# Hybrid decoder layer on one core: layer norm in seven spaced steps, input products and combined blocks at other places of the plan, rotation in four instructions

## The reference, cut to what matters

```
h = rmsnorm(x, norm_g)
p = einsum('btd,dn->btn', h, w_in)          # all branches read one projection
o_a = silu(a_z) * (a_b * dwconv3(a_c * a_u))
rq = rotary(r_q, pos);  rk = rotary(r_k, pos) * 128 ** -0.5
   # rotary: concat([x1*cos - x2*sin, x1*sin + x2*cos]), x1, x2 the halves of the head
o_r = silu(r_z) * head_norm(retention_chunked(rq, rk, r_v, S))
conv_c = dwconv31(glu_v * sigmoid(glu_g)) + bias
o_c = silu(c_z) * silu(layernorm(conv_c, ln_c_g, ln_c_b))
o_m = silu(m_z) * head_norm(sigmoid(m_o) * mlstm_chunked(...))
y = einsum(sum_n sigmoid(g_n) * (o_n @ w_br[n]), w_out);  x + y, final rmsnorm
```

## Time and profile before

| what | value |
|---|---|
| device time, median of 3 runs | 1559.46 us (1557.69 to 1561.15) |
| time of the profiled execution | 1561.5 us |
| span of the profiled execution | 1559.7 us |
| TensorE busy | 1506.2 us, 97% |
| VectorE busy | 916.5 us, 59% |
| ScalarE busy | 497.8 us, 32% |
| GpSimd busy | 673.9 us, 43% |
| mean granted clock of TensorE | 0.984 |

### The profile page before, as it was taken

The page is one execution under the profiler, slowest core; times in us unless marked ns, Lnnn a source line. Parts: engine busy times, 40 slices in busy tenths (PEclk is TensorE's granted clock), DMA queues, the critical chain, the costliest instruction groups (busy, mean ns, idle before and its releaser), DMA issues.

```text
span 1559.7 us, 26832 instructions
## 1 busy us (share of the span) xinstructions
PE 1506.2 (97%) x10433; PEld 1465.7 (94%) x10433; DVE 916.5 (59%) x1796; ACT 497.8 (32%) x989; POOL 673.9 (43%) x488
## 2 busy tenths in 40 slices
PE   8899999999999999989999999999889999999998
PEld 7899999999999999989999999999779999999886
DVE  6552442456767643277787688787654423885532
ACT  5333323222223233233333333333453331221211
POOL 4221212122132231386777677777546754662100
PEclk9999999999999999999999999999999999999999
DMA  4121212122121221312232222222222466655321
GB/s 170 46 96 41 72 40 84 57 69 73 41 73 34 80 79 42 121 50 87 83 100 82 71 74 70 90 79 88 69 91 68 163 206 203 204 182 158 116 81 71
DMA packets 63989, 144.38 MB, mean 93 GB/s; under 512 B 7656, under 2 KB 36344, under 8 KB 63736
## 3 DMA queue, kind: packets, MB, share of 16 engines
q1 hardware_dynamic: 56616, 116.62, 23.1%
q0 software_dynamic: 6048, 21.73, 3.9%
q10 hardware_dynamic: 1200, 4.33, 0.7%
HBM read 107.01 MB, written 35.64 MB: 91 GB/s over the span
## 4 chain that ended last, share of the span: by engine, by line
PE 79%; DVE 14%; issue 2%; ACT 2%; POOL 1%; DMA 0%; DVEq 0%; ACTq 0%; POOLq 0%
PE bank L1132 10%; PE bank L1134 10%; PE bank L1133 10%; PE bank L1083 8%; PE bank L1085 8%; PE bank L1084 8%; PE bank L1150 4%; PE bank L1151 4%; PE bank L1152 4%; PE bank L1339 2%; PE bank L1340 2%; PE bank L1341 2%; DVE xt L1875 1%; PE sums_ps L1280 1%; PE sums_ps L1270 1%
## 5 line engine op out<-in xcount | busy, mean ns | idle before, releaser
L1083 PE MATMUL bank<-h_hi,w_hi 128*128 128x352 f32 x1032 | 346.7, 336 | 7.5 <-DVE h_lo L1854 4.3
L1085 PE MATMUL bank<-h_hi,w_lo 128*128 128x352 f32 x1032 | 334.9, 324 | 0.0
L1084 PE MATMUL bank<-h_lo,w_hi 128*128 128x352 f32 x1032 | 334.5, 324 | 0.0
L1711 POOL TENSOR_TENSOR w_lo<-stage,w_hi 128x1024 fp32r<-128x1024 f32 x45 | 107.8, 2396 | 336.1 <-ACT w_hi L1381 336.0
L1711 POOL TENSOR_TENSOR t_lo<-stage,t_hi 128x512 fp32r<-128x512 f32 x140 | 187.7, 1343 | 142.9 <-ACT t_hi L1381 142.7
L1132 PE MATMUL bank<-h_hi,t_hi 128*128 128x264 f32 x864 | 248.0, 287 | 0.0
L1133 PE MATMUL bank<-h_lo,t_hi 128*128 128x264 f32 x864 | 246.5, 285 | 0.0
L1134 PE MATMUL bank<-h_hi,t_lo 128*128 128x264 f32 x864 | 246.0, 285 | 0.0
L1132 PE MATMUL bank<-c_hi,t_hi 128*128 128x264 f32 x648 | 187.7, 290 | 19.0 <-DVE part L2004 16.8
L1083 PEld LDWEIGHTS bank<-h_hi,w_hi 128*128 128x128 f32 x1032 | 196.8, 191 | 9.0 <-DVE h_lo L1854 4.6
L1084 PEld LDWEIGHTS bank<-h_lo,w_hi 128*128 128x128 f32 x1032 | 197.3, 191 | 0.1
(11 more groups left out here) (341 smaller groups left out, 2881.2 us busy)
## 6 DMA issues: line engine op xcount, KB each, us to landing
stage<-in_wa SPq DMA_DIRECT2D x64, 512.0 KB, 3.4
piece<-g_rows SPq DMA_DIRECT2D x96, 176.0 KB, 2.8
stage<-in_wg SPq DMA_DIRECT2D x32, 512.0 KB, 3.5
g_rows<-sgt SPq DMA_DIRECT2D x112, 132.0 KB, 1.8
o_raw<-o_rows SPq DMA_DIRECT2D x16, 528.0 KB, 6.9
stage<-in_wb SPq DMA_DIRECT2D x32, 256.0 KB, 2.7
xr<-in_xtok SPq DMA_DIRECT2D x9, 512.0 KB, 3.6
xt<-in_xT SPq DMA_DIRECT2D x6, 704.0 KB, 8.6
```

Of the source, the lines that this page charges most:

```text
L1083: pe.matmul(out, hi, h_hi[:, k, tok(b)], start=(k == 0), stop=False)
L1084: pe.matmul(out, hi, h_lo[:, k, tok(b)], start=False, stop=False)
L1085: mm = pe.matmul(out, lo, h_hi[:, k, tok(b)], start=False, stop=(k == KD - 1))
L1711: pool.tensor_tensor(lo, split_src(item), hi.bitcast(F32), ALU.subtract).then_inc(lo_done, 1)
```

## The change

The change has five parts. (1) In the retention phases `comb` moves from slots 1, 3, ..., 11 to 12, 13, ..., 17, and `comb_split` from 14, 16, 18 to 18, 20, 22. In the last phase `comb` 3 moves from 22..27 to 1, 3, ..., 11, `comb_split` to 14, 16, 18 and `comb4` from 31, 33, 35, 37 to 24, 27, 30, 33; attention 7 has stride 1.4 for 1.5. (2) `rotate` takes four instructions for six: a second table `tab2` holds sin and -sin, so that one multiplication and one addition cover all 128 partitions. It is one more DMA in GpSimd's queue, and as `tab2` overlaps the place of a later buffer GpSimd waits there for all attention state updates. (3) GLU 2 and 3 move from windows 9 and 14 to 6 and 10; conv_a and out_a of groups 1 to 3 move with them (out_a 3 to window 19). (4) The slots for taps change: none in slot 0 behind a window that is not a gate pair; behind an `acau` window 2, 6, 10, 11, 12, 13 for 0, 2, 6, 10, 12. Worked out from the lists, tap 1 of the four groups moves from (0, 1), (4, 6), (10, 0), (15, 0) to (0, 1), (5, 1), (9, 6), (14, 6), and `tap_s` from (1, 2), (5, 11), (10, 12), (15, 12) to (1, 6), (5, 13), (10, 6), (15, 5). (5) The layer norm starts at (19, 0), takes seven steps a block, at slots 0 `ln0`, 3 `lnm`, 4 `ln1`, 7 `ln1b`, 10 `lnv`, 11 `lns`, 13 `ln2`, with 14 slots from block to block, and `ln3a` and `ln3` lie five slots apart. Root and inverse stay in PSUM.

```diff
         if h:
             for i in range(6):
-                tasks.setdefault(2 * i + 1, []).append(("comb", h - 1, i))
+                tasks.setdefault(12 + i, []).append(("comb", h - 1, i))
             for c in range(3):
-                tasks.setdefault(14 + 2 * c, []).append(("comb_split", h - 1, c))
+                tasks.setdefault(18 + 2 * c, []).append(("comb_split", h - 1, c))
...
-    tasks = spread(attention(7), 0, 1.5)
+    tasks = spread(attention(7), 0, 1.4)
     for i in range(6):
-        tasks.setdefault(22 + i, []).append(("comb", 3, i))
+        tasks.setdefault(2 * i + 1, []).append(("comb", 3, i))
+    for c in range(3):
+        tasks.setdefault(14 + 2 * c, []).append(("comb_split", 3, c))
     for k in range(4):
-        tasks[31 + 2 * k] = [("comb4", k)]
-    for c in range(3):
-        tasks.setdefault(28 + c, []).append(("comb_split", 3, c))
+        tasks.setdefault(24 + 3 * k, []).append(("comb4", k))
...
-    for what in (glu(1), None, conv_a(0), None, out_a(0), None, conv_a(1), None, out_a(1), glu(2), None, conv_a(2), None,
-                 out_a(2), glu(3), None, conv_a(3), None, out_a(3), None, None, None, None, out_c(0), out_c(2),
+    for what in (glu(1), None, conv_a(0), None, out_a(0), None, glu(2), None, conv_a(1), None, glu(3), None, out_a(1),
+                 conv_a(2), None, out_a(2), None, conv_a(3), None, out_a(3), None, None, None, out_c(0), out_c(2),
...
-        short = bool(pairs) and pairs[-1][0] == "acau"
-        free = {"cvcg": (0, 1, 5, 6, 9, 10, 13), "acau": (0, 1, 2, 5, 6, 9, 10), "abaz": (0, 1, 2, 5, 6)}.get(
-            kind[0], (0, 2, 6, 10, 12) if short else (0, 1, 2, 5, 6, 9, 10, 11, 12, 13))
+        before = pairs[-1][0] if pairs else None
+        free = {"cvcg": (0, 1, 5, 6, 9, 10), "acau": (0, 1, 2, 5, 6, 9, 10), "abaz": (0, 1, 2, 5, 6)}.get(
+            kind[0], (2, 6, 10, 11, 12, 13) if before == "acau" else (0, 1, 2, 5, 6, 9, 10, 11, 12, 13))
+        if before != "g":
+            free = free[1:] if free[0] == 0 else free
...
     for b in range(3):
-        tasks_at(at + 9 * b, ("ln0", b))
-        tasks_at(at + 3 + 9 * b, ("ln1", b))
-        tasks_at(at + 6 + 9 * b, ("ln2", b))
+        for late_by, step in ((0, "ln0"), (3, "lnm"), (4, "ln1"), (7, "ln1b"), (10, "lnv"), (11, "lns"), (13, "ln2")):
+            tasks_at(at + 14 * b + late_by, (step, b))
     for g in range(4):
-        tasks_at(at + 28 + 3 * g, ("ln3", g))
+        tasks_at(at + 42 + 5 * g, ("ln3a", g))
+        tasks_at(at + 44 + 5 * g, ("ln3", g))
...
                 if pair == 0:
+                    if w == 0:
+                        pool.wait_ge(upd_done, 16)
...
-                    pool.dma_start(tab[:, :], rot).then_inc(tab_in, 16)
+                    pool.dma_start(tab[:, :], rot[0]).then_inc(tab_in, 16)
+                    pool.dma_start(tab2[:, :], rot[1]).then_inc(tab_in, 16)
...
-                c, s = tab[0:hw, tok(b)], tab[hw:P, tok(b)]
-                own(TT(dst[0:hw, :], ps[0:hw, :], c, ALU.mult))
-                own(TT(rb[0:hw, :], ps[hw:P, :], s, ALU.mult))
-                own(TT(dst[hw:P, :], ps[0:hw, :], s, ALU.mult))
-                TT(rb[hw:P, :], ps[hw:P, :], c, ALU.mult).then_inc(freed["V"], 1)
-                own.wait()
-                own(TT(dst[0:hw, :], dst[0:hw, :], rb[0:hw, :], ALU.subtract))
+                own(TT(dst[:, :], ps[:, :], tab[:, tok(b)], ALU.mult))
+                own(TT(rb[0:hw, :], ps[hw:P, :], tab2[hw:P, tok(b)], ALU.mult))
+                TT(rb[hw:P, :], ps[0:hw, :], tab2[0:hw, tok(b)], ALU.mult).then_inc(freed["V"], 1)
+                own.wait()
                 dve.wait_ge(freed["V"], n)
-                own(TT(dst[hw:P, :], dst[hw:P, :], rb[hw:P, :], ALU.add))
+                own(TT(dst[:, :], dst[:, :], rb[:, :], ALU.add))
...
             def ln2(b):
                 dve.wait_ge(ln_act, 2 * b + 2)
-                own(dve.reciprocal(lnr[:, :], lnr[:, :]))
+                own(dve.reciprocal(pb[:, 0:BLK], pb[:, 0:BLK]))
                 own.wait()
                 for g in range(4):
-                    own(TT(cc[g][:, tok(b)], cc[g][:, tok(b)], lnr[:, :], ALU.mult))
+                    own(TT(cc[g][:, tok(b)], cc[g][:, tok(b)], pb[:, 0:BLK], ALU.mult))
```

More of the change, by code:

```diff
@@ L202, in make_plan @@
     nw = len(pairs)
-    room[0] = room[0][1:]
     first_pair = {("cvcg", g): w for w, (kind, g, _) in enumerate(pairs) if kind == "cvcg"}
@@ L608, in hybrid_step @@
         kx = at("kx", [P, NB, P], F32, e_at + 544)
+        tab2 = at("tab2", [P, T], F32, e_at + 4640)
         v1 = sb("v1", [P, P + 1])
@@ L1298, in pt, with lnm @@
                     pe.transpose(tb[:, 0:NS], rt[0:NS, CH, 0:P], ident[0:NS, 0:NS]).then_inc(pt_ready, 1)
-            def ln1(b):
+            def lnm(b):
                 pe.wait_ge(pt_used, 24)
@@ L1305, in ln1, with lnv @@
                 pe.matmul(tb[:, 0:BLK], ones[:, :], lnsq[:, 0, :], start=True, stop=True).then_inc(ln_pe, 1)
-            def ln2(b):
+            def lnv(b):
                 pe.wait_ge(ln_dve, 4 * b + 3)
@@ L1312, in _ @@
             walk({"blk": blk, "prod": prod, "pblk": pblk, "m1": m1, "m3": m3, "m4": m4, "m5": m5, "m6": m6, "m7": m7, "mws": mws,
-                  "a": a, "b": b, "as": as_, "bs1": bs1, "bs2": bs2, "pt": pt, "ln1": ln1, "ln2": ln2})
+                  "a": a, "b": b, "as": as_, "bs1": bs1, "bs2": bs2, "pt": pt, "lnm": lnm, "lnv": lnv})
             ring = bank + [tb, pb]
@@ L1637, in ln1, with lns, ln3a @@
                 act.sem_inc(ln_act, 1)
-            def ln2(b):
+            def lns(b):
                 act.wait_ge(ln_pe, 2 * b + 2)
-                act.activation(lnr[:, :], pb[:, 0:BLK], ACT.Sqrt, bias=eps[:, :]).then_inc(ln_act, 1)
-            def ln3(g):
+                act.activation(pb[:, 0:BLK], pb[:, 0:BLK], ACT.Sqrt, bias=eps[:, :]).then_inc(ln_act, 1)
+            def ln3a(g):
                 act.wait_ge(ln_dve, 12 + g)
@@ L1662, in _ @@
                   "mws": mws, "a": a, "b": b, "as": as_, "bs1": bs1, "pr": pr, "tap0": tap0,
-                  "ln1": ln1, "ln2": ln2, "ln3": ln3})
+                  "ln1": ln1, "lns": lns, "ln3a": ln3a})
             act.wait_ge(acc_final, 1)
@@ L2487, in ln1, with ln1b @@
                 dve.sem_inc(ln_dve, 1)
+            def ln1b(b):
                 dve.wait_ge(ln_act, 2 * b + 1)
@@ L2523, in _ @@
                   "a": a, "b": b, "as": as_, "bs1": bs1, "bs2": bs2, "pn": pn, "pr": pr, "pt": pt, "tap": tap,
-                  "ln0": ln0, "ln1": ln1, "ln2": ln2, "ln3": ln3})
+                  "ln0": ln0, "ln1": ln1, "ln1b": ln1b, "ln2": ln2, "ln3": ln3})
             own.wait()
```

9 lines of the change are left out of this document (5 added, 4 removed).

## The result

The changed kernel took 1532.77 us (median of 4 runs, 1531.81 to 1534.89), the kernel before 1560.31 on the same chip; the ratio is 0.9836 with a 95% interval of 0.9813 to 0.9858. It is faster, as forecast, but by 27 us and not by 40: 1532.8 against 1520. (The ratio is not that of the two medians; by it the gain is 25.6 us.)

The account below looks back on a forecast made before the run. The prediction took TensorE, busy 97% of the span, as the bound, plus its waits and lower-clock losses. Gains of -48.0 and costs of +8.5 gave -39.5 against 1559.7, hence 1520 us; range 1508 to 1533.

Parts of the forecast that it names:

- The three waits at `sw`: Retention phases with `comb`: TensorE's waits of 1.98, 1.99, 1.98 us go; with clock and a fourth wait, -11.8 us.
- The gap at 690: Start of the windows: TensorE's wait of 6.71 us for u2 goes, with 2.3 at the lower clock, -9.0 us.
- windows 1 and 10: TensorE's waits for u2 at 715 and 902 go as taps move from early slots, -5.1 us with clock.
- the term of -14.1: Waits for u2 at the start of the windows (-9.0) and in windows 1 and 10 (-5.1), both expected gone.
- The crowded slots: Slots 9 to 13 behind `acau`: VectorE 1.9 us late, nothing added; as a slower rival up to 1579, chance 0.04.
- The norm's term: Layer norm: old waits and clock loss go, -22.1 us; new waits at `lnm` cost +5.4, +1.3 and +0.3.
- The other moves here are hidden: Retention phases: `comb_split`, the second table's DMA and GpSimd's new wait were claimed to cost nothing.
- +1.5: Retention phases: moved `comb` steps between `bs1` and `pr` delay `pt`, 0.5 us a phase, bounds 0 and 1.5.
- TensorE waits 3.7 us, and 1.7 more go at the lower clock: Layer norm, second `lnm`, window 19: VectorE's `ln2` and next `ln0` crowd ahead of it, +5.4 us.
- 1.25: Layer norm, third `lnm`, window 20: the wait in us expected there, entered as +1.3.
- Rival C: Retention phases: every moved `comb` takes 1.7 us, `pt` over 2 us late, clock falls three times, +9.6: 1530; chance 0.12.
- rival B: Layer norm: GpSimd beside each `ln0` and a second late step in two blocks; 1532 us, chance 0.15.

Follow-up runs that it names:

- norm_slots_back: The changed kernel with the layer norm's steps back at their old slots, its cheaper functions kept; 16 us more than the changed kernel by the medians.
- last_phase_only: The kernel before with only the last attention phase's `comb`, `comb_split` and `comb4` moves, spacing still 1.5; ratio 0.9985 to the kernel before.
- old_windows: norm_slots_back with the windows' old pair order and free slots as well; 5.5 us more than norm_slots_back by the medians.
- splits_late: The changed kernel with the last head's `comb_split` at slots 20, 21, 22 instead of 14, 16, 18; 2.8 us less than the changed kernel by the medians.
- no_gpsimd_low: The changed kernel with GpSimd's three `c_lo` subtractions of the last head left out, zeros written instead; 4.5 us less than the changed kernel by the medians.
- wm_early: The changed kernel with `wm` and the copy `qm` made one chunk earlier; median 1532.64 us against 1532.77.
- repaired: The changed kernel with phase 1 to 3 `comb` steps and splits moved, the last head's splits later, `wm` and `qm` one chunk earlier; 1521.01 us, ratio 0.9748.

## Why the prediction was right in part and wrong in size

**Right.** TensorE's work stayed. The three waits at `sw` fell from 1.98 to 0.34 with the clock at 1.00. The gap at 690 went to 0.55 and windows 1 and 10 to none. Against the term of -14.1 norm_slots_back has 15.3 us less in the windows than before, its cheaper multiplications included; the split into 9.0 and 5.1 was wrong, as last_phase_only and old_windows show. The crowded slots cost nothing: no wait for u2 in any window from 686 to 1089, though `tap_s` of two groups stands at (10, 1) and (15, 0), in the early slots that the prediction had it leave.

**Right by luck in part.** The norm's term is -22.1 + 7.0 = -15.1, and norm_slots_back gives 13.0. But the 7.0 was worked out for places that the kernel doesn't have: with the norm starting at (18, 11) the products' steps around `ln2` and `ln0` are not those of P3 in window 19 that the sum used. And its two parts missed in opposite directions: 5.4 was 2.73, 1.3 was 5.0.

**The step that failed most** is "The other moves here are hidden: `comb_split` has idle ScalarE and GpSimd", which the prediction applied to the last phase as well: there, "A wait of 0.9 us at 616 I leave as it is" and "`comb_split` 3 stands in slot 18, ahead of the window's weight work". GpSimd was idle, but its instruction holds up VectorE's `pr`: 3.78 us of wait, 3.0 at the lower clock, and 1.85 more at `bs1` (2.78 for 0.93). That is the 8.6 us of the last phase. splits_late and no_gpsimd_low show the first two, wm_early the third. repaired, with the causes taken away, has 100.0 us there. What the prediction asked of a moved step on GpSimd, whether the engine is free, was the wrong question.

**A term mis-sized** is "+1.5", `comb` between `bs1` and `pr`: 4.55. In the changed kernel two `comb` steps take 3.53 us together at 431.62 beside a `w_lo` of 432.11, with a third behind them; over the kernel their line has a mean of 1224 ns where the earlier trace rows has 708. The waits of 1.61, 1.48 and 1.46 lie at the upper bound of 1.5 a phase, one of them over it; the value of 0.5 was too low, though the earlier trace rows had the longer duration. With the 0.34 left at each `sw` (1.0 in all) this is 4.1 of the 4.7 us missing in the phases.

**The norm**: "TensorE waits 3.7 us, and 1.7 more go at the lower clock" was 2.73 and none; the third, "1.25", was 3.34 and 1.7 of clock, as the second block's root came 4.73 us after VectorE was free for it. With `lnv`'s 0.9 the sum was 8.6 for 7.0. Rival C had the right place of the second fault and too high a price; rival B ended at the right time, 1532, by another mechanism, which is luck. None of the rivals had GpSimd beside `pr`.

## What to carry to other kernels

When a GpSimd instruction moves, look at what VectorE does in its new slots: each instruction there that works in SBUF alone (an addition of two SBUF inputs, a TENSOR_SCALAR from SBUF to SBUF) stood in these traces until GpSimd's ended, however small it was, while one that reads PSUM did not. Put such splits beside PSUM work, and take small SBUF constants (`wm`) out of the critical chain. And two waits on the same late engine can't simply be added: with the first removed the second was longer here (5.15 us for 2.09), so an edit is priced with its neighbours or not at all.
